# Rows of the experts' ends through SyncE, the next norm inside the embedding, and unit-matrix products in three stages of a two-layer decoder trunk

## What is computed

```python
for i in range(2):                       # DEPTH
    a = rmsnorm(h, norm_mix[i])
    h = h + (even_mixer(a) if i == 0 else odd_mixer(a))
    h = h + hier_moe(rmsnorm(h, norm_ffn[i]))      # each token: 2 of 32 experts
    gate = sigmoid(rmsnorm(h, ple_norm[i]) @ ple_w_gate[i] + ple_b_gate[i])
    h = h + gate * (p[i] @ ple_w_proj[i])          # the embedding
```

## Time and profile before

| | us |
|---|---|
| median of 3 runs | 3158.64 |
| range of the runs | 3158.44 to 3161.94 |
| the profiled execution | 3159.78 |
| its span, first to last instruction | 3158.2 |
| TensorE busy | 2916.5 |
| VectorE busy | 1128.2 |
| ScalarE busy | 652.6 |
| GpSimd busy | 243.5 |
| mean granted clock of TensorE, as a share of full | 0.959 |

### The profile page before, as it was taken

How to read it: one execution, slowest core, us unless ns; L and a number is a source line. 1 busy time by engine, 2 the same in 40 slices (tenths; PEclk the granted TensorE clock), 3 DMA queues, 4 the chain that set the end, 5 groups by cost and what they waited for, 6 DMA issues and landing times. The chain is left out here.

```text
span 3158.2 us, 32607 instructions
## 1 busy us (share of the span) xinstructions
PE 2916.5 (92%) x12473; PEld 1569.3 (50%) x12474; DVE 1128.2 (36%) x2460; ACT 652.6 (21%) x1258; POOL 243.5 (8%) x352
## 2 busy tenths in 40 slices
PE   7999899999799999979979899877997999999798
PEld 5544555555444444424467644477654444444243
DVE  2585355544300000005364635566563000000052
ACT  3310355521100010103021124322211010100030
POOL 0000000001100000011000000043201000000110
PEclk9999999999799999989989899988997999999899
DMA  4000791031599999964020110000416999999630
GB/s 157 27 27 0 309 384 54 1 116 67 214 419 417 413 404 403 390 249 170 40 78 1 16 68 27 0 2 23 161 54 238 410 421 414 406 405 394 247 150 40
DMA packets 138547, 617.21 MB, mean 195 GB/s; under 512 B 25188, under 2 KB 31748, under 8 KB 121992
## 3 DMA queue, kind: packets, MB, share of 16 engines
q1 hardware_dynamic: 110952, 525.93, 42.3%
q0 software_dynamic: 24064, 86.00, 7.2%
q10 hardware_dynamic: 3376, 3.19, 0.3%
HBM read 508.00 MB, written 105.91 MB: 194 GB/s over the span
## 5 line engine op out<-in xcount | busy, mean ns | idle before, releaser
L1994 PE MATMUL acc<-wg,xt 128*128 128x512 f32 x512 | 223.6, 600 | 0.0
L2590 PE MATMUL acc<-xt,work 128*128 128x512 f32 x384 | 166.9, 593 | 0.0
L757 PE MATMUL acc<-h,xt 128*128 128x512 f32 x384 | 165.2, 592 | 0.0
L1994 PEld LDWEIGHTS acc<-wg,xt 128*128 128x128 f32 x512 | 98.6, 193 | 123.7 <-issue 123.7
L396 PE MATMUL scores<-qkt 65*128 65x512 f32 (+7 forms) x384 | 147.9, 495 | 0.9 <-DVE qkt L536 0.9
L542 DVE TENSOR_REDUCE nmax<-scores 128x1 f32<-128x256 f32 (+7 forms) x128 | 96.8, 756 | 76.5 <-PE scores L398 74.4
L1740 PE MATMUL py<-place 128*64 128x512 f32 (+1 forms) x352 | 120.2, 595 | 1.0 <-DVE place L1820 1.0
L1740 PE MATMUL pu<-place 128*128 128x512 f32 (+1 forms) x320 | 119.8, 593 | 0.0
L757 PEld LDWEIGHTS acc<-h,xt 128*128 128x128 f32 x384 | 72.9, 190 | 91.1 <-issue 90.9
L2590 PEld LDWEIGHTS acc<-xt,work 128*128 128x128 f32 x384 | 72.0, 190 | 86.1 <-issue 86.1
L1263 PE MATMUL acc<-place 128*128 128x512 f32 x256 | 112.7, 594 | 1.1 <-PEq L64 1.1
(11 more groups left out here) (638 smaller groups left out, 5145.0 us busy)
## 6 DMA issues: line engine op xcount, KB each, us to landing
own<-in_moe_w_gate_dram SPq DMA_DIRECT2D x22, 2048.0 KB, 16.7
place<-in_moe_w_down_dram SPq DMA_DIRECT2D x22, 2048.0 KB, 16.3
place<-in_moe_w_up_dram SPq DMA_DIRECT2D x20, 2048.0 KB, 17.8
slots_out<-zeros SPq DMA_DIRECT2D x4, 9216.0 KB, 62.9
place<-in_moe_w_gate_dram SPq DMA_DIRECT2D x18, 2048.0 KB, 20.9
own<-in_moe_w_up_dram SPq DMA_DIRECT2D x16, 2048.0 KB, 16.1
own<-in_moe_w_down_dram SPq DMA_DIRECT2D x10, 2048.0 KB, 19.4
xt<-in_moe_w_gate_dram SPq DMA_DIRECT2D x9, 2048.0 KB, 23.0
```

What stands on the lines that cost most here:

```text
L757: last = pe.matmul(acc[:, n % 4, 0:width], xs[:, k, tile_of(i)], weights[:, k, cols], start=(k == 0), stop=(k == k_of - 1))
L1994: last = pe.matmul(acc[:, u % 4, :], xt[:, k, i * P:(i + 1) * P], wg[:, k, n * SLAB:(n + 1) * SLAB], start=(k == 0), stop=(k == KD - 1))
L2590: last = pe.matmul(acc[:, n % 4, :], slabs[m // 4 % 2][:, k, (m % 4) * P:(m % 4 + 1) * P], xt[:, k, half * SLAB:(half + 1) * SLAB], start= ...
```

## The change

It has three parts.

**Transfers at the experts' ends.** The loads of the first two units' rows move from the end of GpSimd's stream of `mixer_end` to the end of SyncE's, with semaphores of their own (`first_in`). The write of the last unit's results in `first_blocks` moves from GpSimd to SyncE, which waits for it (`last_out`); GpSimd waits for the two units before it.

**The next norm.** `rmsnorm_transpose` is gone. `layer_embedding` of layer 0 does its work tile by tile, in the loop over the 16 units: ScalarE squares a tile once it is finished, takes the root and copies half of the turned tile, VectorE makes mean, inverse and scaled tile and copies the other half, TensorE turns it after the product of a later unit. `xt` and `s5_t` are held by `trunk` from the first embedding on; two of the four gather buffers lie in `s5_t` (`later`), and the scaled tiles in the other two (`own_rows`). SyncE brings in the next norm's gains and the first weight slab of the odd mixer when all rows are combined. In layer 1 none of this work is done, but the stage's ten new semaphores are there.

**Unit-matrix products.** `keep_busy` issues products of the unit matrix with itself, 128 columns each, into a PSUM bank whose content is not read: 2 after each of the first eight `turn_qk`, 18, 14, 8 and 10 in the tail of `mixer_end` (both layers), 24 and 10 in `s5_chunks`.

```diff
+def keep_busy(pe, c, bank, count):
+    for _ in range(count):
+        pe.matmul(bank[:, 0:P], c.ident[:], c.ident[:], start=True, stop=True)
...
 (attention)
                 for g in range(8):
                     turn_qk(0, g)
+                    keep_busy(pe, c, po, 2)
...
 (mixer_end, SyncE)
                 bring_in(nc, sp, own_loads, z["own_in"])
+                sp.wait_ge(c.scattered, (layer + 1) * 16 * 2 * NT)
+                for n in range(2):
+                    sp.dma_start(m[:, n, :], c.slots_in[units[n][0] * REGION:units[n][0] * REGION + P, :]).then_inc(c.first_in[n], 16)
...
 (mixer_end, TensorE)
+                keep_busy(pe, c, o_bank, 18)
                 rank_tokens(NT - 2)
                 turn(NT - 1)
                 score(NT - 1)
+                keep_busy(pe, c, o_bank, 14)
                 rank_tokens(NT - 1)
...
+                keep_busy(pe, c, o_bank, 8)
                 pe.wait_ge(z["sorted_at"], 1)
...
                 pe.matmul(turned[:, 1, EXPERTS:2 * EXPERTS], over_wide, earlier, start=True, stop=True).then_inc(z["spread_out"], 1)
+                keep_busy(pe, c, o_bank, 10)
...
 (mixer_end, GpSimd)
-                pool.wait_ge(c.scattered, (layer + 1) * 16 * 2 * NT)
-                for n in range(2):
-                    pool.dma_start(m[:, n, :], c.slots_in[units[n][0] * REGION:units[n][0] * REGION + P, :]).then_inc(c.x_in[n], 16)
...
 (first_blocks, SyncE)
+                sp.wait_ge(y_act, n + 1)
+                sp.wait_ge(y_dve, n + 1)
+                for a, q in enumerate(units[n]):
+                    sp.dma_start(c.slots_out[bass.ds(expert[q] * P, rows), :], y[a * rows:(a + 1) * rows, n % 2]).then_inc(last_out, 16)
+                sp.wait_ge(last_out, 16 * len(units[n]))
...
 (layer_embedding, TensorE, behind the product of unit u)
+                    if next_gain is not None and n == 0 and i >= 2:
+                        next_turn(i - 2)
+                if next_gain is not None:
+                    next_turn(NT - 2)
+                    next_turn(NT - 1)
...
 (layer_embedding, ScalarE, behind the sigmoid of unit u)
+                        if u % 2 == 0 and u >= 2:
+                            next_square(u // 2 - 1)
+                        if u % 2 and u >= 5:
+                            next_copy((u - 5) // 2)
+                        if u % 2 and u >= 3:
+                            next_root((u - 3) // 2)
...
 (layer_embedding, VectorE)
                     add_bias(u)
                     if u:
                         add(u - 1)
+                    if next_gain is not None and u % 2:
+                        if u >= 5:
+                            next_copy((u - 5) // 2)
+                        if u >= 3:
+                            next_scale((u - 3) // 2)
                 add(UNITS - 1)
+                if next_gain is not None:
+                    next_scale(NT - 1)
+                    next_copy(NT - 2)
+                    next_copy(NT - 1)
...
 (s5_chunks)
+                    if k == 2:
+                        keep_busy(pe, c, pz[:, 0], 24)
                     if 1 <= k <= 4:
                         sum_up(2 * k - 2)
...
+                keep_busy(pe, c, pa[:, 0], 10)
                 outputs(NB - 2)
                 outputs(NB - 1)
```

More of the change, by code:

```diff
@@ L1124, in constants @@
     c.x_in = [ctx.enter_context(nc.semaphore(f"x_in{n}")) for n in range(2)]
+    c.first_in = [ctx.enter_context(nc.semaphore(f"first_in{n}_{next(NUMBER)}")) for n in range(2)]
     c.y_out = [ctx.enter_context(nc.semaphore(f"y_out{n}")) for n in range(2)]
@@ L1936, in _ @@
                     sp.dma_start(bias[:], row(t["ple_b_gate"][layer]).to_broadcast([P, D])).then_inc(bias_in, 16)
+                if next_gain is not None:
+                    sp.wait_ge(combined, NT)
+                    sp.dma_start(next_gains, row(next_gain).to_broadcast([P, D])).then_inc(next_gain_in, 16)
+                    with nc.allow_non_contiguous_dma(reason="weights' column slabs"):
+                        for tile, view in loads:
+                            sp.dma_start(tile, view).then_inc(loaded, 16)
                 for i in range(NT):
```

187 lines of the change are left out of this document (77 added, 110 removed).

## The result

The changed kernel takes 3114.68 us (median of 4 runs, 3113.26 to 3120.56), against 3159.95 for the kernel before (4 runs, 3158.44 to 3161.94). The ratio is 0.986, with a 95% interval of 0.9843 to 0.9877. The forecast was 3116.7, in a range of 3104 to 3136. The span of the profiled execution went from 3158.2 to 3111.7, so 46.5 shorter, where the sum had 41.9. (The profiled execution of the changed kernel, of 3113.26, is the fastest of its four.)

A forecast was written before the change was run, and what follows sets the result against it. TensorE was taken as the bound, busy 2916.5 of 3158.2 us at mean clock 0.959. The terms summed to 41.9 off the profiled 3159.8, so 3117.9, median 3116.7, range 3104 to 3136.

The forecast's parts named there:

- last results through SyncE: End of the experts: SyncE writes the last results, so GpSimd's drain no longer holds the barrier; 5.0 us per layer, 10.0 saved.
- first rows through SyncE: Start of the experts: SyncE loads the first rows, so TensorE starts 3.2 us earlier in each layer; 6.4 saved.
- next norm: Between the last gate product and the odd mixer: the norm moves into the embedding's loop; 12.5 us saved.
- `attention`: Start of `attention`: unit products fill gaps so that TensorE runs at full clock; 3.4 us saved.
- unit products, tail of `mixer_end`: Clock falls again between 18 and 14; part of the gain at the experts' start remains: 0.8 us per layer, 1.6 saved.
- `s5_chunks` and behind: The 10 save 7.0 us and 0.5 in the stage behind, the 24 in the gap of 7.91 save 1.1: 8.6.
- Rival 3: End of `mixer_end`: GpSimd's drain behind the scatter takes 14.9 us, the 6.4 saving becomes a 12.2 loss: 3135.3; chance 0.08.
- the 1.6 worked out from it: Both transfer places, both layers: if only the queues' first-byte times differed, 1.6 us saved, the whole near 3131.5.
- The chain of 12.7: From the last gate bias to the odd mixer's first product, the last tile's steps take 12.7 us, against 30.7 before.
- The cover: In the embedding's loop: ScalarE's 5.9 and VectorE's 6.4 us per tile hide under 14.0, so the norm costs only the transposes.
- the 0.24 and the 0.13: Tail of `mixer_end`: us per instruction in the 14's row; 0.24 is the sign of half clock, 0.13 of clock held.
- Rival 1: Tail of `mixer_end`: the clock holds throughout, 11.0 us there in place of 1.6: 3106.6 in all; chance 0.15.

The follow-up runs named there:

- e1: The kernel before with only the transfers of the experts' ends moved to SyncE: 3145.76 us against 3159.78.
- e2: The kernel before with only the next norm moved inside the embedding: 3147.01 us, 12.8 less.
- e4: The changed kernel without the ten unit products behind the last product of `mixer_end`: 3115.71 us.
- e5: The changed kernel without the 18, 14 and 8 unit products in the tail of `mixer_end`, the ten kept: 3114.41 us.
- e12_later_start: The changed kernel with eight more unit products as TensorE's first work of `s5_glu`: 3118.40 us.
- e8: The changed kernel with the last tile's transposes ahead of the ranks in the tail of `mixer_end`, and other numbers of unit products: 3107.18 us.
- e10: The changed kernel with e8's tail (5 unit products last), semaphores cleared by ranges, no 24, and 18 and 11 unit products in the embedding: 3100.06 us.
- e11: e10 with 28 more unit products in `s5_chunks` ahead of the third group of `sum_up`: 3100.46 us.
- e3_units: The kernel before with only the unit products of the change: 3145.28 us, 14.5 less.

## Why the prediction was right

The time and the sum held, but in part because errors on either side cancelled. Term by term, from the two traces (predicted, measured):

| step | predicted | measured |
|---|---|---|
| last results through SyncE | 10.0 | 7.1 |
| first rows through SyncE | 6.4 | 5.7 (e1), hidden by the ten |
| next norm | 12.5 | 14.4 (13.1 alone, e2; 1.3 by the clock) |
| `attention` | 3.4 | 3.4 |
| unit products, tail of `mixer_end` | 1.6 | 4.9 |
| `s5_chunks` and behind | 8.6 | 5.7 + 3.6 |
| joint stage behind the norm | 0 | 1.4 |
| semaphores at the end | −0.6 | −0.9 |
| other | 0 | 1.2 |
| sum | 41.9 | 46.5 |

The measured 4.9 of the tail is what remains of both layers' `mixer_end`, experts and the small stage behind them (18.3) after the terms for the transfers and 0.6 for the small stage. By the runs it is 2 × 1.4 for the ten (e4) and 2 for the other forty (e5). That the median came within 2 us of the forecast is luck as far as the terms go: two were 3 off, one too high and one too low, and 2.6 came by position.

- *Last results.* The mechanism was right, the size was 3 too high. The landing took 2.6 as taken from the earlier trace rows. The issue of two transfers took 1.5, from the copy's end to 1391.3, where I had 0.5 from a row of one transfer. The 37 clears took 2.6 and not 2.1: 0.07 each by their row, where the earlier trace rows had 0.058.
- *First rows.* 3.2 per layer predicted, 3.0 and 2.7 measured, with the transfers' landing late next, as the prediction said. Its price for the drain was too high: the row of 5.7 begins before the last scatter is issued, and ends 3.3 behind it, not 5.1. That changed nothing, since SyncE and VectorE are ready later. Rival 3 (a drain of 14.9 like that of the earlier trace rows) is refuted by the row at 818.4.
- By the Trainium skill, "DMA: Bandwidth & Descriptors", section "Specifications", the queues differ by about 0.4 in their first byte. The seams of the runs went by the 5.1 of the drain and by the clears instead: e1 brought 14.0, not the 1.6 worked out from it.
- *Next norm.* The chain of 12.7 was 12.4. The transposes inside the loop cost about the 5.5 that I took: in e2 it is 169.3 from the embedding's start to its last gate product, where it was 164.1, so 5.2. In the changed kernel it is 168.0, so 3.9, since the clock is at half for the first 9.9 us of the embedding there, and for 14.8 or 14.9 before and in e2. That is the 1.3 between 13.1 and 14.4, by this comparison. The cover held as said: VectorE is busy for 76.8 and ScalarE for 63.2 of those 168.0. The 1.4 in the joint stage was priced at nothing; e1 has it without the norm, so it goes with the clock's position.
- *Attention.* Right in mechanism and size: the 10.2 us at half clock are gone. `attention` takes 336.6 or 336.7 in all eleven kernels with the unit products, and 340.1 to 342.0 in the three without.
- *Tail of `mixer_end`.* The forecast that the clock falls between the 18 and the 14 and that the last ten reach over the barrier is what the rows show (half clock in 808.9 to 812.6; 3.3 late). The 14 ran at half for only a part: 4.64 for 28 instructions, 0.17 each, between the 0.24 and the 0.13 that I had named as signs. The step that failed is the price of the experts' start: I gave 0.8 per layer for what is a whole stretch at full clock. By e4 the ten bring 4.7 there (3.6 of clock, close to the 3.5 of my upper bound, and 1.1 of landing that they cover) and cost 3.3, so 1.4, and the forty before them bring 1 more.
- *`s5_chunks`.* The term was mis-sized in two ways that cancelled. The 24 were placed in the wrong gap, which a reading of the order around line 2385 would have told. The half clock in the middle came once more, in front of the fourth `sum_up`, and cost 1.4 (87.2, against 85.7 to 85.9 in eight of the nine other kernels with the ten). And 3.6 came from two stages behind, for which I had 0.5; 2.6 of them hang on a shift of 1.9 us (e12_later_start).

Rival 1, the clock held through the tail, was not what the change does, but e8 shows that another order can bring it about. The Trainium skill ("TensorE: Matmul & The Clock Gate", section "Why this matters for your kernels") wants idle stretches kept short; e8 agrees with it, at 1.00 over 23.5 us with no gap over 1. It is not the whole story: in e10's layer 0 the same order, with gaps just as short, had the clock at half in 810.0 to 813.4. Of the six tails of this order that were traced (two each in e8, e10 and e11), four kept the clock. And the changed kernel, whose forty fillers leave gaps of 1.8 us behind the 18 and of up to 1.2 behind the 8, did not keep it, and gained 1 us per layer by them (e5).

## What to carry to other kernels

Look at the end of each stage for the engine that is ready last, and at what stands behind its last real work: a software queue's drain (5 us here) or a row of small clears (2.6 us) is worth as much as a faster product. Unit products paid where they end just as a long run of work begins (4.7 for 3.3 at the experts, some 7 for the ten in `s5_chunks`). Filling the gaps of a whole stretch, together with another order, brought 5.7 in the traced execution of e8 and did not hold the clock every time; filling some of them brought next to nothing. When a change shifts the program in time, a stage without an edit may change by 1 or 2% by the clock alone, and a fall that is prevented at one place may come at the next (e11), so differences of 3 us between two kernels need a look at the stages' lengths before they are put down to an edit.

## What the runs showed of the hardware

GpSimd's drain behind indirect scatters begins, in the trace, before the last of them is issued and ends 3.3 us behind it, but behind 16 gathers it takes 14.9; behind two plain transfers it was 5.1, and 4.96 in the changed kernel, where it is off the path. A clear of one semaphore is 25 ns long in its row, but 37 of them take 2.6 us, and one instruction clears a whole range in 71 or 106 ns. Runs of one kernel on one chip lie up to 15 us apart (e3_units, 3133.07 to 3147.81), while the delta rule's stage is 163.4 to 164.1 in nine kernels with the ten and 166.0 to 166.3 in four without (and in e12_later_start): the clock's part in the time is repeatable at some places and not at others.
